# Gated linear recurrence: decay factors multiplied up from fine to coarse blocks in place, instead of exponentials of differences of summed logarithms

## The reference, cut to what matters

```python
log_f = jnp.log(lb + (1.0 - lb) * jax.nn.sigmoid(f_pre))       # forget factor per token and channel
k_in  = (1.0 - lb) * jax.nn.sigmoid(-f_pre)
q_in  = jax.nn.silu(hg_q)
def step(state, inp):                                          # one chunk of BLOCK = 128 tokens
    qc, kc, vc, gc = inp
    bc = jnp.cumsum(gc, axis=2)
    decay = jnp.exp(jnp.where(causal, bc[:, :, :, None, :] - bc[:, :, None, :, :], -jnp.inf))
    scores = jnp.einsum('bhtd,bhsd,bhtsd->bhts', qc, kc, decay)
    o = jnp.einsum('bhts,bhsv->bhtv', scores, vc) + jnp.einsum('bhtd,bhdv->bhtv', qc * jnp.exp(bc), state)
    b_last = bc[:, :, -1, :]
    state = jnp.exp(b_last)[..., None] * state + jnp.einsum(
        'bhsd,bhsv->bhdv', kc * jnp.exp(b_last[:, :, None, :] - bc), vc)
    return state, o
o_hg = rmsnorm_per_head(o) * gain * jax.nn.silu(hg_g)
```

## Time and profile before

| what | us |
|---|---|
| time, median of 3 runs | 2378.21 (2378.13 to 2389.55) |
| the profiled execution's own time | 2376.62 |
| its span, first to last instruction | 2374.8 |
| attention block | 225.4 to 322.6 |
| recurrence block | 322.6 to 410.2 |
| PE / DVE / ACT / POOL busy over the whole span | 88% / 60% / 46% / 8% |

### The profile page before, as it was taken

How to read it: one execution, slowest core, us unless ns; L and a number is a source line. 1 busy time by engine, 2 the same in 40 slices (tenths; PEclk the granted TensorE clock), 3 DMA queues, 4 the chain that set the end, 5 groups by cost and what they waited for, 6 DMA issues and landing times. The chain is left out here.

```text
span 2374.8 us, 25271 instructions
## 1 busy us (share of the span) xinstructions
PE 2083.6 (88%) x10228; PEld 1664.6 (70%) x10228; DVE 1415.8 (60%) x1560; ACT 1085.1 (46%) x1232; POOL 185.7 (8%) x132
## 2 busy tenths in 40 slices
PE   5999965766999999993889999997698987999997
PEld 4887655664666666662778888886577866888786
DVE  4112788357998898885159888887643345333213
ACT  4233632216888888874235544444242224222212
POOL 0001031001222222210000000000000000000000
PEclk9999888857999999996789999998899998999999
DMA  4220000406999999984133333313122222333231
GB/s 144 83 72 1 1 1 21 169 36 238 403 406 402 403 405 399 402 344 156 40 107 89 89 89 93 104 54 107 37 88 89 89 86 65 98 97 92 85 107 53
DMA packets 202060, 346.86 MB, mean 146 GB/s; under 512 B 13871, under 2 KB 149543, under 8 KB 184535
## 3 DMA queue, kind: packets, MB, share of 16 engines
q1 hardware_dynamic: 191280, 332.49, 39.8%
q0 software_dynamic: 5120, 8.40, 1.1%
q10 hardware_dynamic: 5543, 4.34, 0.6%
HBM read 340.93 MB, written 12.65 MB: 149 GB/s over the span
## 5 line engine op out<-in xcount | busy, mean ns | idle before, releaser
L1465 DVE TENSOR_TENSOR wlo_e<-raw_e,whi_e 128x2048 fp32r<-128x2048 f32 x192 | 436.4, 2288 | 57.9 <-ACT whi_e L1387 57.2
L1387 ACT CAST whi_e<-raw_e 128x2048 fp32r<-128x2048 f32 x192 | 366.7, 1912 | 72.9 <-PE pall L1548 32.1
L1768 DVE TENSOR_TENSOR w_lo<-w_raw,w_hi 128x2048 fp32r<-128x2048 f32 x89 | 203.8, 2289 | 321.1 <-ACT w_hi L1760 321.1
L48 PE MATMUL pall<-hT_hi,w_lo 128*128 128x512 f32 x864 | 347.9, 403 | 23.1 <-DVE xbc L2312 10.3
L1760 ACT CAST w_hi<-w_raw 128x2048 fp32r<-128x2048 f32 x89 | 169.4, 1904 | 428.9 <-PE pall L50 414.6
L49 PE MATMUL pall<-hT_lo,w_hi 128*128 128x512 f32 x864 | 341.9, 396 | 0.0
L50 PE MATMUL pall<-hT_hi,w_hi 128*128 128x512 f32 x864 | 341.4, 395 | 0.0
L1547 PE MATMUL pall<-whi_e,xs 128*128 128x512 f32 x512 | 208.9, 408 | 10.1 <-DVE xs L1471 5.2
L48 PEld LDWEIGHTS pall<-hT_hi,w_lo 128*128 128x128 f32 x864 | 166.0, 192 | 60.0 <-DVE xbc L2312 10.6
L1548 PE MATMUL pall<-wlo_e,xs 128*64 128x512 f32 x512 | 204.9, 400 | 0.0
L49 PEld LDWEIGHTS pall<-hT_lo,w_hi 128*128 128x128 f32 x864 | 166.0, 192 | 35.0 <-issue 0.5
(11 more groups left out here) (495 smaller groups left out, 3941.2 us busy)
## 6 DMA issues: line engine op xcount, KB each, us to landing
raw_e<-in_w_expert_up_dram SPq DMA_DIRECT2D x64, 1024.0 KB, 11.2
raw_e<-in_w_expert_down_dram SPq DMA_DIRECT2D x64, 1024.0 KB, 11.8
raw_e<-in_w_expert_gate_dram SPq DMA_DIRECT2D x64, 1024.0 KB, 11.7
w_raw<-in_w_in_dram SPq DMA_DIRECT2D x80, 512.0 KB, 5.9
w_raw<-in_w_gate_up_dram SPq DMA_DIRECT2D x44, 512.0 KB, 5.1
w_raw<-in_w_down_dram SPq DMA_DIRECT2D x22, 512.0 KB, 4.1
mixed<-in_w_in_dram SPq DMA_DIRECT2D x10, 1024.0 KB, 5.0
A<-acs_rows SPq DMA_DIRECT2D x8, 1024.0 KB, 4.8
```

What stands on the lines that cost most here:

```text
L48: nc.tensor.matmul(out, w_lo, m_hi, start=start, stop=False)
L1387: nc.scalar.copy(whi[j][:, :], raw[j][:, :]).then_inc(sem_hi, 1)
L1465: nc.vector.tensor_tensor(wlo[j][:, :], raw[j][:, :], whi[j][:, :].bitcast(F32), ALU.subtract).then_inc(sem_lo, 1)
L1768: (engine or self.nc.vector).tensor_tensor(self.lo[i][:, :], self.raw[i][:, :], self.hi[i][:, :].bitcast(F32), ALU.subtract).then_inc(self ...
```

## The change

**In the projection block** the masks are built for six thresholds and in another order (diagonal first, then w = 1, 2, ...); the last one takes all pairs of w = 32 and w = 64.

**In the attention block** ACT's logarithm becomes a linear map (the forget factor itself, same shape and count). DVE's `decays` becomes `keys`, one scaling of `sgn` in place per head and no scans. POOL's four memsets go; in their place POOL waits for the fourth forget factor and then multiplies `q1` = `hqT` x forget (2048 elements), and seven tables `decay[2]` to `decay[128]`, each the product of neighbouring pairs of the one before. The tiles `qz`, `kz`, `kx`, `bx` are gone, and the attention has buffers of its own.

**In the recurrence block** the sizes go from fine to coarse. Queries and keys are multiplied in place, head by head: after the product of size w, the right half of each pair of blocks in `q1` takes the product of the left block's factors, the left half in `sgn` that of the right block. There are no exponents, exponentials, key factors on POOL or cleared buffers but `acc`. The last product (w = 64) is a 64x64 corner written over its bank, so that it and w = 32 share one `select`. After the last multiplication `q1` and `sgn` hold the decays to the chunk's start and end, which the outputs and the transposes use. The norm reads PSUM: ACT squares with a running sum (16 instructions), and one DVE instruction per head and chunk scales by the root and by the gate.

```diff
-                def log_forget(e):
-                    nc.scalar.activation(lf[:, e, :], hfT[:, e, :], ACT.Ln, bias=lb[:, e:e + 1],
+                def forget(e):
+                    nc.scalar.activation(hfT[:, e, :], hfT[:, e, :], ACT.Identity, bias=lb[:, e:e + 1],
...
-                for t in (qz[0], kz[0]):
-                    gp.memset(t[:, :], 0.0)
+                pool.wait_ge(s["f"], HG_HEADS)
+                gp.tensor_tensor(q1[:, :, :], hqT[:, :, :], hfT[:, :, META:TM], ALU.mult).then_inc(s["q1"], 1)
+                for i, w in enumerate((2, 4, 8, 16, 32, 64, 128)):
+                    if i >= 1:
+                        pool.wait_ge(s["dec"], i)
...
+                    gp.tensor_tensor(decay[w][:, :, :], pairs[:, :, :, 0], pairs[:, :, :, 1], ALU.mult).then_inc(s["dec"], 1)
...
-                def decays(e):
-
-                    V.tensor_scalar(km[:, e, :], sgn[:, e, 0:META], omlb[:, e:e + 1], None, ALU.mult)
-                    V.tensor_scalar(kx[:, e, :], sgn[:, e, META:TM], omlb[:, e:e + 1], None, ALU.mult).then_inc(s["kx"], 1)
-                    dve.wait_ge(s["rst"], 2)
-                    dve.wait_ge(s["lf"], e + 1)
-                    V.tensor_tensor_scan(bm[:, e, :], ones[:, 0:META], lf[:, e, 0:META], 0.0, ALU.mult, ALU.add)
...
+                def keys(e):
+                    V.tensor_scalar(sgn[:, e, :], sgn[:, e, :], omlb[:, e:e + 1], None, ALU.mult).then_inc(s["kx"], 1)
...
+            SPANS = [0, 1, 2, 4, 8, 16, 32, 64]
+            LAST = len(SPANS) - 1
...
+                def products(lv, e):
+                    n = lv * HG_HEADS + e
+                    if lv >= 2:
+                        pe.wait_ge(s["fac"], n - 2 * HG_HEADS + 1)
...
+                        if n >= 8:
+                            pe.wait_ge(s["acc"], n - 7)
+                        q = hqT if lv == 0 else q1
+                        for c in range(NT):
+                            last = nc.tensor.matmul(pall[:, level_bank(lv, e), c * P:c * P + P],
+                                                    sgn[:, e, META + c * P:META + c * P + P], q[:, e, c * P:c * P + P],
+                                                    start=True, stop=True)
...
+                def factors(lv, e):
+                    w = SPANS[lv]
+                    dve.wait_ge(s["sc"], lv * HG_HEADS + e + 1)
...
+                    V.tensor_tensor(k, k, dk.to_broadcast([P, (TM - first) // (2 * w), w]), ALU.mult)
+                    V.tensor_tensor(q, q, dq.to_broadcast([P, T // (2 * w), w]), ALU.mult).then_inc(s["fac"], 1)
...
+                for lv in range(1, LAST):
+                    for e in range(HG_HEADS):
+                        if lv >= 2:
+                            dve.wait_ge(s["fac"], (lv - 2) * HG_HEADS + e + 1)
+                        factors(lv, e)
+                        if lv != LAST - 1:
+                            select(lv, e)
...
+                    for e in range(HG_HEADS):
+                        last = V.scalar_tensor_tensor(mixed[:, c, 512 + e * P:512 + e * P + P],
+                                                      pall[:, (6 + c) % 8, e * P:e * P + P], rs[:, c, e:e + 1],
+                                                      hg_nat[:, c, e * P:e * P + P], ALU.mult, ALU.mult)
...
+                        nc.scalar.activation(sqo[:, :], pall[:, (6 + c) % 8, e * P:e * P + P], ACT.Square,
+                                             accum_out=ssq[:, c, e:e + 1]).then_inc(s["sq"], 1)
```

More of the change, by code:

```diff
@@ L437, in stage_a @@
         s = {n: sem("b_" + n) for n in (
[L438 removed]
+            "zm z ab u l k q t w o oev con conr qs qhi own vb kb vr vm abm um lm spm tm wm om mo osq ossq ort ors on f kx q1 dec tab").split()}
         with ExitStack() as tmp:
@@ L442, in stage_a @@
             qh, ql = ([sb(f"{n}{i}", [P, WIDTH], F32R, ctx=tmp) for i in range(2)] for n in ("qh", "ql"))
-            ww = [qz[1][:, 0:WIDTH], kz[1][:, 0:WIDTH]]
+            ww = [sb(f"ww{i}", [P, WIDTH], ctx=tmp) for i in range(2)]
             lm, spm, wm = (sb(n, [P, T], ctx=tmp) for n in ("lm", "spm", "wm"))
@@ L447, in stage_a @@
             pick = sb("pick_m", [META, SB_HEADS, META], ctx=tmp)
-            from_on, before, own_head = (qz[1][:, WIDTH + i * P:WIDTH + i * P + P] for i in range(3))
-            into_head = kz[1][:, WIDTH:WIDTH + 2 * P - META]
+            consts = sb("consts", [P, 5 * P - META], ctx=tmp)
+            from_on, before, own_head = (consts[:, i * P:i * P + P] for i in range(3))
+            into_head = consts[:, 3 * P:5 * P - META]
             from_on_r, before_r = (sb(n, [P, P], F32R, ctx=tmp) for n in ("from_on_r", "before_r"))
@@ L596, in _ @@
                     if 2 <= n < 2 + HG_HEADS:
-                        log_forget(n - 2)
+                        forget(n - 2)
                 act.wait_ge(s["tm"], SB_HEADS + 1)
@@ L707, in _ @@
                     if 6 <= n < 6 + HG_HEADS:
-                        decays(n - 6)
+                        keys(n - 6)
                 out_evacuate(SB_HEADS - 1)
@@ L902, in products @@
                     last.then_inc(s["sc"], 1)
-                for n in range(HG_HEADS * (LEVELS + 1)):
-                    products(n)
-                pe.wait_ge(s["acc"], HG_HEADS * (LEVELS + 1))
-                pe.wait_ge(s["kd"], 1)
+                for lv in range(LAST + 1):
+                    for e in range(HG_HEADS):
+                        products(lv, e)
+                pe.wait_ge(s["acc"], 4 * HG_HEADS + HG_HEADS + 1)
                 for e in range(HG_HEADS):
-                    last = nc.tensor.transpose(pall[0:META, 0, e * P:e * P + P], kdm[:, e, :], ident[:, :])
+                    last = nc.tensor.transpose(pall[0:META, 4, e * P:e * P + P], sgn[:, e, 0:META], ident[:, :])
@@ new lines, in _ @@
+            @block.scalar
+            def _(act):
+                act.wait_ge(s["kdt"], 1)
+                nc.scalar.copy(kdnm[:, :, :], pall[0:META, 4, :].rearrange("p (e d) -> p e d", e=HG_HEADS)).then_inc(s["kdn"], 1)
+                for c in range(3):
+                    act.wait_ge(s["kdt"], c + 2)
+                    nc.scalar.copy(kdn[:, c, :, :], pall[:, 5 + c, :].rearrange("p (e d) -> p e d", e=HG_HEADS)).then_inc(s["kdn"], 1)
+                for c in range(NT):
+                    act.wait_ge(s["os"], c + 1)
+                    for e in range(HG_HEADS):
+                        n = c * HG_HEADS + e
+                        if n >= 1:
+                            act.wait_ge(s["sq"], n)
+                        nc.scalar.activation(sqo[:, :], pall[:, (6 + c) % 8, e * P:e * P + P], ACT.Square,
+                                             accum_out=ssq[:, c, e:e + 1]).then_inc(s["sq"], 1)
+                    act.wait_ge(s["sq"], (c + 1) * HG_HEADS)
+                    nc.scalar.activation(rt[:, c, :], ssq[:, c, :], ACT.Sqrt, bias=eps[:, 0:1],
+                                         scale=1.0 / HG_DIM).then_inc(s["rt"], 1)
@@ L938, in stage_a, with _ @@
+            @block.gpsimd
+            def _(pool):
+                g["sweep"](pool)
+                nc.gpsimd.memset(acc, 0.0).then_inc(s["cleared"], 1)
         g["clear"](s)
```

252 lines of the change are left out of this document (76 added, 176 removed).

## The result

The changed kernel takes 2349.24 us (median of four runs, 2346.69 to 2357.24), the kernel before, on the same chip, 2378.36 (2378.13 to 2389.55): a ratio of 0.988 with the interval 0.985 to 0.990, and 29.1 us less. The forecast was 2349.0 us, 29.5 us less. The profiled execution happened to be the longest of the four (2357.24 us, span 2355.4). It lost some 8 us once among the experts, at 582 us, as told at the end. The blocks that the change touches are therefore read by themselves.

A forecast was written before the change was run, and what follows sets the result against it. The prediction took DVE to bound most of the recurrence and PE the attention, with a stall and low clock; -30.7 us (recurrence) and +1.2 us (attention) gave -29.5 us, 2348.7 us, rounded to 2349, range 2337 to 2361 us.

The forecast's parts named there:

- PE begins at once; DVE's first factors 6.7 us later: Recurrence start: PE's products need only what the attention left; head 0 of size 1 is done 6.7 us after the start.
- A size is 5.24 us: Recurrence size loop: DVE's two multiplies and a select for four heads take 5.24 us a size, 26.2 us for five.
- The products hide: Recurrence sizes: PE's product, 0.94 us a head at full clock, stays hidden behind DVE's 1.31 us.
- The second rival: Recurrence: PE runs at half the clock and becomes the bound, 15.6 us more, 2364 us; chance 0.12.
- 16 multiplies, 5.5 us: Recurrence, last two sizes: no select between them, so DVE does 16 multiplies in 5.5 us.
- The chain, 9.3 us: Recurrence, decayed keys to first output chunk: same matmuls, copies and state updates, so the 9.30 us of before.
- The norm, 9.0 us: Recurrence end: ACT squares from PSUM and DVE scales, 9.0 us instead of 14.80.
- Sum of the recurrence, -30.7 us: Whole recurrence block: it ends 30.7 us earlier, at 379.5 instead of 410.2 us.
- Attention, +1.2 us: Attention block: POOL's multiplies hold DVE, a 9.7 us delay less the 8.5 us lost before, net 1.2 us later.
- POOL holds nothing: Rival, attention: POOL's multiplies don't hold DVE, so stall and low clock vanish, 8.5 us gained, 2339 us; chance 0.10.
- POOL's tables are slow: Rival, attention: strided tables hold DVE far longer; from 17 ns per element the kernel is slower than before; chance 0.02.
- The clock falls twice: Rival, attention: PE's clock falls a second time, 6 us more, 2355 us; chance 0.08.

The follow-up runs named there:

- e4: Changed kernel with the selects of sizes 1 to 16 cut to 8 of 128 columns per chunk (most scores left out, timing only); 2344.44 us, ratio 0.987.
- e1: Changed kernel with POOL's eight attention multiplies (q1 and seven tables) started only after DVE's last piece of the attention; 2337.11 us, ratio 0.984.
- e3: Changed kernel with the norm of the kernel before (DVE copies, squares, sums and scales; ACT takes only the root); 2355.63 us, ratio 0.991.
- e9: Changed kernel run once more without any edit, for a second profile; 2355.41 us, one run.
- e8: e1 with the query half of the recurrence's multiplies, sizes 1 to 16, moved from DVE to POOL; 2332.1 us, ratio 0.980.
- e5: Changed kernel with POOL's query multiply (q1) in the attention done twice in a row; 2359.27 us, ratio 0.991.
- e6: Changed kernel with only POOL's query multiply (q1) moved behind DVE's last piece of the attention, tables left in place; 2340.74 us, ratio 0.982.
- e11: e8 plus PE's products of sizes 0 and 1 alternating by head, with DVE's selects and factors in the same order; 2334.61 us, ratio 0.981.

## Why the prediction was right, and where a term was off

- **PE begins at once; DVE's first factors 6.7 us later.** Measured 6.4. Right.
- **A size is 5.24 us.** DVE's factors and selects of five sizes ran from 332.02 to 357.8 us, 5.16 each. Right, and with it the assumption that multiplies of 256 elements in place, every second one at w = 1, keep their price (0.42 us in all rows).
- **The products hide.** DVE is busy in 31.28 of 31.30 us, and e4 shows the margin: PE alone would need 0.89 us a head where DVE needs 1.29. The second rival (PE at half the clock) did not occur; the granted clock was 1.00 from 332 us to the end of the norm.
- **16 multiplies, 5.5 us.** Measured 5.4.
- **The chain, 9.3 us.** This term was mis-sized: 8.1. I took the old duration unchanged, but it had been measured at a mean clock of 0.84 and ran now at 1.00. The rows below show where: the twelve transposes at the chain's head took 2.82 us at a clock of 0.50 before and 1.50 at 1.00 now, and in e1, where the clock was 0.52 there, again 2.71. I had argued for the full clock in the rivals and not applied it here.
- **The norm, 9.0 us.** Measured 8.9, with ACT's pitch of 0.40 us for a square and its read, and 0.28 us a multiply on DVE. Right; e3 puts the norm's share of the gain at 5.7 us by taking its edit out.
- **Sum of the recurrence, -30.7 us.** Measured -32.7: 1.2 from the chain, the rest in tenths from the others.
- **Attention, +1.2 us.** Measured +3.8 in the profiled execution, +2.3 of it in the stall (10.8 against 8.5 us). The other 1.5 us lie before the first `values` (21.5 instead of 20.0 us), with more low clock at the block's start; the second profile of the kernel before has the 21.5 too, so they are not the change's. The mechanism was as stepped through: the cast held to the end of the query multiply, the subtract to the end of the first table, the late copy. Two things in it were not. The first wait was 2.40 us and not 3.6: from the start of POOL's query multiply to the end of DVE's subtract 7.2 us went by where I had 8.35 (multiplies of 4.55 and 2.13 us instead of 4.8 and 2.5, and no gap between them). And the clock did not fall there but 5 us later, behind the second wait, so that `values` of the third head came 4.7 us late and not 6.8, and the low clock was spent on what followed. The two errors nearly cancel in that execution, and that was luck: e9 shows the same program with 7.3 us more.
- **The rivals.** "POOL holds nothing" is refuted by two rows and its time of 2339 us is what e1 reached by moving the multiplies (2337.1). "POOL's tables are slow" is refuted: they read every second element at 2.0 ns per element (2.13 us for 1056), no more than the 2.2 of the query multiply without strides (4.55 us for 2048). "The clock falls twice" was priced at 2355 us; e9 has about that time with one long fall, and the profiled run too, but by the experts. I gave it 0.08 as if it were one outcome for the kernel. It is a spread between profiles of one program, and should have widened the forecast's own case instead.

The chain's transposes, in the timelines of the kernel before, the changed kernel and e1:

```profile
386.18 2.82 PE L915 MATMUL pall<-ident,kz 128*128 128x128 f32 x12 [1.10 <-DVE kz L837]
```

```profile
363.40 1.50 PE L782 MATMUL pall<-ident,sgn 128*128 128x128 f32 x12 [1.56 <-DVE q L816]
```

```profile
352.71 2.71 PE L783 MATMUL pall<-ident,sgn 128*128 128x128 f32 x12 [1.56 <-DVE q L817]
```

The total came out within 0.3 us of the forecast because the recurrence won 2.0 us more than I had and the attention's stall cost 1.1 us more in the profiled execution; the rest is below what single runs of this kernel differ by (2346.7 to 2357.2 us). So close an agreement is luck as well: the profiled execution was 8 us above the median for a loss among the experts, and how long the low clock lasted in the three executions without a profile isn't known.

## What to carry to other kernels

Moving work to POOL "because it is idle" is not free while DVE works between SBUF tiles: ask what DVE does in those microseconds and who waits for it. Here eight multiplies of 10.5 us cost 10.5 to 18.1 us where PE waited for DVE, and nothing 44 us later in the same block. Twenty small ones (e8) pay inside the recurrence, where DVE reads PSUM meanwhile. A wait of PE should be priced with the low clock that may follow, which in these profiles cost 1.5 to 19 times the wait itself (6.4 us for 4.4, 11.1 for 0.57). Whether a stall is there has to be read from a profile: whole runs differ by as much for other reasons. A duration taken from a stretch at low clock must be converted before it goes into a sum for a stretch at full clock.

## What the runs showed of the hardware that I had not expected

- After a wait of only 0.57 us PE ran at 1.2 GHz for 24 us with no idle time of its own, in two profiles of two; in the kernel before, 2.40 us were followed by 14 us. The length did not follow the wait.
- The same instructions at the same place, with the same first wait, had 14, 17, 17 and 34 us of it in four profiles (the changed kernel, e3, e4, e9). A single profile is not the kernel where the clock has a part.
- The expert stage has a loss of its own that comes and goes. In the profiled run of the changed kernel one row gather's issue on POOL lasted 11.65 us, where the gathers around it last 0.9 to 2.8, and PE then waited 10.41 us for it:

```profile
582.13 11.65 POOL L1459 DMA_INDIRECT xg<-m_rows,row_x  x1 [0.30 <-issue]
...
599.91 1.41 PE L1488 MATMUL pall<-ident,xg 128*128 128x128 f32 x8 [10.41 <-DMA xg<-m_rows,row_x]
```

The lead on the kernel before shrank from 29.7 us at the first gather to 22.1 at the last. e3, e5, e6 and e11 have one such issue of 7.25 us in the same place, the other nine profiles none above 3.4. All have the DMA engines close to fully busy there, so what decides it stays open; no run was made for it.
